# ScalarE takes both PSUM copies of the filter's odd transforms in a Hyena and windowed-attention encoder layer

## The reference, cut to what matters

```python
def implicit_filter(L, f_w1, f_b1, f_freq, f_w2, f_b2, f_w3):
    ...
    h = jnp.sin(freq * (z @ f_w1.astype(f32) + f_b1.astype(f32)))
    h = jnp.sin(freq * (h @ f_w2.astype(f32) + f_b2.astype(f32)))
    h = h @ f_w3.astype(f32)
    ...
    h = h.reshape(L, 2, HY_CH) * decay[:, None, :]
    return h[:, 0], h[:, 1]

def bidir_long_conv(u, h_f, h_b, d_skip):
    ...
    K = jnp.fft.rfft(k, axis=0)
    y = jnp.fft.irfft(U * K[None], n=2 * L, axis=1)[:, :L]
```

## Time and profile before

| what | value |
|---|---|
| time, median of 3 runs | 2929.34 us (2928.68 to 2930.3) |
| time of the profiled execution | 2931.11 us |
| its span in the profile | 2929.3 us |
| mean granted TensorE clock | 0.979 of full speed |
| PE busy | 2784.7 us (95% of the span) |
| DVE busy | 1880.4 us (64%) |
| ACT busy | 1216.7 us (42%) |
| POOL busy | 1014.2 us (35%) |

### The profile page before, as it was taken

The page is one execution under the profiler, slowest core; times in us unless marked ns, Lnnn a source line. Parts: engine busy times, 40 slices in busy tenths (PEclk is TensorE's granted clock), DMA queues, the critical chain, the costliest instruction groups (busy, mean ns, idle before and its releaser), DMA issues.

```text
span 2929.3 us, 38413 instructions
## 1 busy us (share of the span) xinstructions
PE 2784.7 (95%) x14352; PEld 2517.9 (86%) x14352; DVE 1880.4 (64%) x2590; ACT 1216.7 (42%) x1923; POOL 1014.2 (35%) x870
## 2 busy tenths in 40 slices
PE   6988899999897999998999999999999999999999
PEld 5877898888786788887899999899999989999998
DVE  6765566778565666666666665766666576666665
ACT  5553554544454766675332322333232233323221
POOL 1112121133211344345454543435454343433432
PEclk9999999999997999999999999999999999999999
DMA  6475998886796335334332232432223243221221
GB/s 208 131 235 165 270 260 235 262 239 178 213 264 162 107 109 130 109 113 161 115 91 90 83 94 76 161 134 87 91 83 99 70 168 129 63 76 55 83 65 69
DMA packets 391553, 405.32 MB, mean 138 GB/s; under 512 B 46270, under 2 KB 327230, under 8 KB 391079
## 3 DMA queue, kind: packets, MB, share of 16 engines
q1 hardware_dynamic: 359496, 322.50, 37.5%
q0 software_dynamic: 31872, 80.36, 8.4%
HBM read 292.14 MB, written 110.64 MB: 138 GB/s over the span
## 4 chain that ended last, share of the span: by engine, by line
PE 83%; DVE 5%; ACT 4%; issue 3%; DMA 3%; POOL 1%; SPq 0%; DVEq 0%; POOLq 0%; ACTq 0%
PE ff_banks L85 11%; PE ff_banks L87 11%; PE ff_banks L86 11%; PE ff_down L85 6%; PE ff_down L86 6%; PE ff_down L87 6%; PE pr_acc L85 4%; PE pr_acc L86 4%; PE pr_acc L87 4%; PE pr_gen L85 3%; PE pr_gen L87 2%; PE pr_gen L86 2%; PE am_mix L85 2%; PE am_mix L86 2%; PE am_mix L87 2%
## 5 line engine op out<-in xcount | busy, mean ns | idle before, releaser
L2617 POOL TENSOR_TENSOR ff_alo_raw<-ff_alo_raw,ff_silu 128x384 f32<-128x384 f32 x132 | 196.0, 1485 | 702.7 <-DVE ff_alo_raw L2840 627.3
L2862 DVE TENSOR_TENSOR ff_h<-ff_h,ff_down 128x512 f32<-128x512 f32 x396 | 264.9, 684 | 160.0 <-PE ff_down L87 157.0
L85 PE MATMUL pr_acc<-pr_xhi,pr_whi 128*128 128x386 f32 (+1 forms) x864 | 310.1, 359 | 25.8 <-DVE pr_xlo L1434 25.8
L85 PE MATMUL ff_banks<-ff_xhi,ff_ghi 128*128 128x384 f32 x924 | 315.0, 341 | 13.3 <-DVE ff_glo L2850 7.6
L85 PE MATMUL ff_down<-ff_dhi,ff_ahi 128*128 128x512 f32 x792 | 313.0, 395 | 3.5 <-issue 3.5
L87 PE MATMUL ff_banks<-ff_xhi,ff_glo 128*128 128x384 f32 x924 | 313.1, 339 | 0.0
L86 PE MATMUL ff_down<-ff_dlo,ff_ahi 128*128 128x512 f32 x792 | 313.0, 395 | 0.0
L87 PE MATMUL ff_down<-ff_dhi,ff_alo 128*128 128x512 f32 x792 | 312.8, 395 | 0.0
L86 PE MATMUL ff_banks<-ff_xlo,ff_ghi 128*128 128x384 f32 x924 | 311.9, 338 | 0.0
L86 PE MATMUL ff_banks<-ff_xlo,ff_uhi 128*128 128x384 f32 x924 | 311.0, 337 | 0.0
L85 PE MATMUL ff_banks<-ff_xhi,ff_uhi 128*128 128x384 f32 x924 | 310.7, 336 | 0.0
(11 more groups left out here) (298 smaller groups left out, 6563.9 us busy)
## 6 DMA issues: line engine op xcount, KB each, us to landing
ff_glo_raw<-w_gate_up SPq DMA_DIRECT2D x132, 256.0 KB, 3.0
ff_ulo_raw<-w_gate_up SPq DMA_DIRECT2D x132, 256.0 KB
ff_dlo_raw<-w_down SPq DMA_DIRECT2D x66, 512.0 KB, 4.4
pr_raw<-w_in SPq DMA_DIRECT2D x108, 256.0 KB, 6.0
f_dram<-fi_out POOLq DMA_DIRECT2D x32, 512.0 KB, 4.2
fs_a<-f_dram SPq DMA_DIRECT2D x32, 512.0 KB, 9.0
pr_xs<-x SPq DMA_DIRECT2D x18, 512.0 KB, 5.7
xkeep_dram<-pr_xs SPq DMA_DIRECT2D x18, 512.0 KB, 4.7
```

What stands on the lines that cost most here:

```text
L85: pe.matmul(out, still[0], moving[0], start=start, stop=False)
L2617: pool.tensor_tensor(block(prod, c), block(prod, c), silu[c][:], ALU.mult).then_inc(tempered, 1)
L2862: dve.tensor_tensor(h[j][:, o], h[j][:, o], down(v), ALU.add).then_inc(added, 1)
```

## The change

For the odd transforms of the long sequence (w = 1, 3, ..., 31, sixteen of them) ACT copies bank 2 and then, after a wait for the second group of matmuls, bank 3; it counts `copied_v` itself. DVE skips its part for these. Even transforms and the two of the short sequence stay as they were.

```diff
+    def whole(w):
+
+        return w % 2 == 1 and w < 2 * N2
...
             act.copy(out[:, w % 2, 0, :], gen[:, 2, :]).then_inc(copied_a, 1)
+            if whole(w):
+                act.wait_ge(spectral, 2 * w + 2)
+                act.copy(out[:, w % 2, 1, :], gen[:, 3, :]).then_inc(copied_v, 1)
...
         def part_out(w):
+            if whole(w):
+                return
             dve.wait_ge(spectral, 2 * w + 2)
             if w >= 2:
                 dve.wait_ge(stored[w % 2], 16 * (w // 2))
```

## The result

| | before | after |
|---|---|---|
| median of the runs | 2929.3 us | 2912.9 us (2909.6 to 2918.7, 6 runs) |
| ratio | 1 | 0.9947 (95% interval 0.9933 to 0.996) |
| profiled execution: time, span | 2931.1, 2929.3 us | 2912.2, 2910.4 us |

The ratio is a gain of 15.5 us (11.7 to 19.6). The changed kernel was run once more later, as `again`, with 0.995 (0.9933 to 0.9968).

The account below looks back on a forecast made before the run. The filter's stage was taken as bound by a loop through several engines, PE elsewhere; 9.0 + 1.9 + 1.25 - 0.5 + 1.5 - 1.5 = 11.65 us off 2929.3 gave 2917.7 us, range 2915 to 2921.5 (8 in 10: 2910.5 to 2925.5).

Parts of the forecast that it names:

- What bounds the stage: Filter's stage, 160 to 285 us: a loop through several engines, DVE's copy late behind `hlo` and two weightings.
- The stalls: PE's eight waits for DVE's copy of bank 3, 8.2 us plus restarts, go: 9.0 us gained after corrections.
- Store and table: POOL's odd store and table load go earlier, ending PE's stalls at 200.30 and 287.40: 1.9 and 1.25 us gained.
- ACT's copies: Sixteen more copies in ACT's queue, covered by idle time except at 174.58 us: 0.5 us lost.
- The clock: Slow matmuls behind idle times in four places, at most 6.4 us, partly regain full pace: 1.5 us gained.
- the next late store: The even transform's store, behind POOL's multiplication, becomes late and delays the even copies: 1.5 us lost.
- A: Rival, chance 0.18: idle times shrink enough that all four slow spells go; gain 16.6 us, 2912.8 us.
- B: Rival, chance 0.17: even stores or the `hlo` wait take half back, tables stay late; about 5 us remain, 2924 us.
- C: Rival, chance 0.07: the time won is given back at a DMA-fed stage, 312 to 440 us; 2929 us.
- D: Rival, chance 0.06: ACT's queue becomes the late one, up to 9.4 us with nothing gained; 2938.7 us.

Follow-up runs that it names:

- dve_first: The kernel before, with DVE's odd copy moved to the head of its weigh_step, ahead of `hlo` and the two weightings; ratio 0.9966 to before.
- the ghosts: The kernel after plus sixteen unread DVE multiplications where the odd copies stood: 0.9936 of before with nobody waiting, 0.9998 with PE and POOL waiting.
- late_store: The kernel after, with POOL waiting for the step's weighting before the odd store; ratio 0.9944 to before.
- act_twice: The kernel after, with ACT copying bank 3 of each odd transform twice; ratio 0.994 to before.

## Why the prediction was right, and where it was off

The sum, laid beside the evictions. I placed its terms by the times of the stalls in the profile before:

| part of the stage | predicted | measured, after | measured, `again` |
|---|---|---|---|
| eviction 2 to 6: one stall | -1.3 | -1.1 | -1.2 |
| 6 to 9: what was left of a stall, and ACT's copy | -0.35 + 0.5 | +1.5 | -0.4 |
| 9 to 11: the first table | -1.9 | -3.6 | -3.7 |
| 11 to 17: six stalls | -7.35 | -8.6 | -10.1 |
| 17 to 19: the second table | -1.25 | -4.0 | -2.5 |
| 19 to the next stage | 0 | +0.7 | +1.2 |
| clock and late even stores, not placed | -1.5 + 1.5 | in the rows above | in the rows above |
| sum | -11.65 | -15.1 | -16.7 |

**What bounds the stage**: right. It is a loop through DVE's queue, and in it the copy that stood behind `hlo` and the weightings; `dve_first` and the ghosts show the order, and not the work, to be the cause.

**The stalls**: right. In the turn used as the example `made` was to begin 1.28 us sooner; the turn is 1.23 us shorter (11.24 to 10.01 us between evictions). The six turns took 67.9 us, the forecast said about 60, and they take 59.3. Of these 8.6 us 1.6 are the slow matmuls at 214 us, which are gone; stalls and restarts gave 7.0 where 7.35 stood.

**Store and table**: the places were right, the sizes too small. From eviction 9 to 11 the stall of 1.92 us went, and with it the slow matmuls behind it: nine took 3.7 us from 200.30 on, where nine take 2.1 at 2.4 GHz. From 17 to 19 the stall of 1.25 us went, and fourteen matmuls behind it, 5.5 us from 287.40 on where they take 3.0. The reason given, that ACT's earlier copy sends store and table off earlier, is not borne out as the whole of it. Counted from eviction 9 the store went out 2.5 us sooner, as forecast, but the table behind it also took 5.3 us instead of 8.8. And `late_store` holds store and table back and loses 0.2 us of the 7.6 at the two places. So these stalls hang on PE's order or on the transfers' durations as well; how they divide is not settled, because the durations change with every order.

**ACT's copies**: the place was right, the cost there is not settled. It is 1.5 us in the profile after, since the store that ACT waits for landed no earlier although everything before it had been won earlier; in `again` the stretch is 0.4 us shorter than before. Elsewhere they cost nothing that can be seen, as `act_twice` shows.

**The clock, 1.5 us, and the next late store, -1.5 us**: this is the step that was mis-sized, and most of the 3.5 us by which the sum is short come from it. Of the four slow spells three went, those at 200, 214 and 287 us; the one at 258 us stayed, at 248.6 in the profile after. Beside the pace at 2.4 GHz the three had taken 1.6, 1.6 and 2.6 us more, 5.8 in all, where 1.5 were forecast. The granted clock from 160 to 190 us reads 0.89 instead of 0.94, but most of that lies in PE's longer idle time there: three matmuls of 512 columns are slow behind it, where five were. And the even stores, which were to take 1.5 us away, never became late enough: ACT waits 10.2 us for stores instead of 12.0, and PE 0.4 us for ACT. That the time came out near A's and not near 2917.7 is mostly this term's doing. Which spells stay differs between the two profiles of the change (last section), so the rows of before could not have told it.

**Rivals.** A, with 2912.8 us, describes the measured 2912.9 better than the forecast of 2917.7; its mechanism, the clock staying up, took place in three spells of four. That its number is met to 0.1 us is luck: one spell stayed, and other terms were off by 1 us and more. B, another stall in place of the old one, took place at 175 us alone, and in `again` not there either. C fell: the gain went through the DMA-fed stage from 312 us on, of 15.0 us at its start 13.8 are there at the attention. D fell with `act_twice`.

## What to carry to other kernels

Before moving a copy to another engine, ask not which engine is less busy but what stands ahead of the copy in each queue at the moment its source is ready: DVE's copy took 0.68 us and cost 1.2 us in a turn with a stall, because it stood behind three instructions of DVE's queue that took 2.6 us:

```profile
233.59 1.22 DVE L1518 TENSOR_TENSOR fi_hlo<-fi_h,fi_hhi 128x1024 fp32r<-128x1024 f32 x1
234.94 0.69 DVE L1524 TENSOR_TENSOR fi_h<-pr_gen,fi_dec 128x512 f32<-128x512 f32 x1
235.55 0.68 DVE L1529 TENSOR_TENSOR fi_h<-pr_gen,fi_dec 128x512 f32<-128x512 f32 x1
236.15 0.68 DVE L1507 COPY fi_out<-pr_gen 128x512 f32<-128x512 f32 x1
```

A ghost, an instruction of the same length in the same place, once awaited and once not, separates the price of the signal from the price of the work in two runs. Where stalls pull the clock down, count the slow matmuls behind each stall with it: here they were over a third of the gain.

## What the runs showed of the hardware

Equal idle times did not have equal consequences for TensorE's clock. In the profile after, PE was idle for 1.95 us before 209.34 and the matmuls that followed kept 0.23 us; the same idle time before 247.15 was followed by matmuls 0.43 us apart from 249.18 on, at the 1.2 GHz level:

```profile
209.34 0.47 PE L85 MATMUL pr_gen<-fi_hhi,fi_table 128*128 128x512 f32 x1 [1.95 <-issue]
...
247.15 0.47 PE L85 MATMUL pr_gen<-fi_hhi,fi_table 128*128 128x512 f32 x1 [1.95 <-issue]
...
249.18 0.63 PE L86 MATMUL pr_gen<-fi_w3lo,fi_fhi 128*128 128x512 f32 x1
249.61 0.63 PE L87 MATMUL pr_gen<-fi_w3hi,fi_flo 128*128 128x512 f32 x1
```

In `again`, the same kernel, PE idled 1.96 us before the same instruction and no slow matmul followed; its six turns took 57.7 us instead of 59.3. But `again` has seven matmuls 0.43 us apart from 267.60 on, behind an idle time of 2.20 us, where the profile after has none behind 2.22 us at 273.47:

```profile
266.33 0.50 PE L85 MATMUL pr_gen<-fi_hhi,fi_table 128*128 128x512 f32 x1 [2.20 <-DVE fi_hlo L1527]
...
268.01 0.63 PE L85 MATMUL pr_gen<-fi_hhi,fi_table 128*128 128x512 f32 x1
268.44 0.63 PE L86 MATMUL pr_gen<-fi_hlo,fi_table 128*128 128x512 f32 x1
```

So from 190 us to the next stage each profile of the change has one such spell, worth 1.6 us, but at another place. The Trainium skill (TensorE: Matmul & The Clock Gate, "Part 1: The HAM clock gate") says of a kernel's first matmuls that one and the same kernel can show different numbers of slow ones from run to run; these two profiles show the like in the middle of a kernel.

ACT's issue of a 512 KB store took 0.33 us of its queue, POOL's 0.54 us. The same store took 6.41, 7.69 and 5.80 us to land in the profiles of before, after and `again`.
